# Two PSUM banks for the turned rows of the output projections, three projection weights loaded a stage ahead, another load order in the second attention, and the gate terms of the mLSTM moved into the first attention

## Chip, cores and metric

The kernel runs on 1 core of a Trainium2 chip, as one launch. The metric is the device time of that launch in microseconds (us); smaller is better.

## What is computed

Two transformer blocks, one after the other, on 2048 tokens of width 1024, all in float32. Only the parts that the change touches are given.

```python
# first block: windowed attention and a two-way mLSTM side by side, one output projection, expert-choice FFN
att = latent_attention(q, k, v, k_ctx, v_ctx, sink)        # 8 heads, blocks of 128, window 128, 256 context keys
st_f = mlstm_state_update(zero, cmk, cmv, cli_f, clf_f)    # two context chunks give the first state, each way
h_sum = bidir_mlstm(mq, mk, mv, li_f, lf_f, li_b, lf_b, st_f, st_b)      # 16 chunks of 128 tokens each way
mix = concatenate([att, mlstm_out(h_sum, mo, mlstm_norm_w)])
x = x + g1 * (mix @ w_out)                                 # w_out 1024 x 1024
hx2 = modulate(rmsnorm(x, norm2_w), sh2, sc2)              # goes to the router and the experts
# mLSTM state step
b = cumsum(lf); w = b[-1] - b + li; m_new = max(b[-1] + m, w.max())
C_new = exp(b[-1] + m - m_new) * C + einsum('s,sd,sv->dv', exp(w - m_new), k, v)
# second block
proj = h @ w_in                                            # w_in 1024 x 1472
attn = mla_attention(...)                                  # 4 heads, causal, 2048 x 2048, head width 128 + 64
x = x + gate1 * (concatenate([rms_norm(attn), rms_norm(lru)]) @ w_out)
h2 = rms_norm(x, norm2_g) * (1 + scale2) + shift2          # router and 32 experts follow
```

## The kernel before

The program is a row of stages, each with its own buffers and a barrier of all engines at its end: `inp1` (first projection), `att` (windowed attention), `ml` (mLSTM), `out1` (first output projection), `choose` (expert choice), `moe1`, `inp2` (second projection), `lata` (second attention), `out2`, `route`, `moe2`. In every stage each engine has its instruction stream written out in Python, and semaphores set the order between the streams. SP issues nearly all loads, in the order in which they are written; POOL issues the stores.

**Output projections** (`out_projection`, used for `out1` and `out2`). The 2048 tokens are 16 tiles of 128 rows. For a tile t, PE multiplies the turned mixed rows `mixT` by `w` into `psO` (L1889, 16 matmuls, each in two passes in the trace). DVE adds the residual and normalizes into `xn`; PE turns `xn` by eight 128x128 transposes into `psX` (L1907), four (one "half") into the single bank at a time; ACT evicts each half with scale and shift into `h2T` (L1873); PE multiplies `h2T` by the router weights (`psL`, L1915). One step of the PE stream is: product of tile n+1, turn of the mixed rows of tile n+2 (`psM`), router product of n-1, turn of `xn` of tile n. The second half of a tile waits until ACT has evicted the first:

```python
for q in range(2):
    if not (isinstance(t, int) and t == 0 and q == 0):
        pe.wait_ge(h2T_ready, 2 * t + q)
```

The stage loads `w` itself: eight DMAs of 512 KB on SP, then the router weights `wr` and the gate row `gr`, all on one semaphore `w_landed`, for which the first product waits.

**mLSTM.** `GateColumns` computes, from the 16 gate columns of all 18 chunks (`gate_rows`, left in SBUF by `inp1`), cumulative sums, running maxima and exponents: `chain` on DVE, `products` on PE, `exponents` on ACT, at the start of the stage `ml`. The four context steps (two chunks, both ways) then follow one another through one PSUM tile `psC` and the state `C`, and then the 32 steps of the scan.

**First attention.** Per block of 128 queries and per group g of four: scores in `psS` (single buffer), a minimum on DVE (L1173), exp on ACT (L1218), turn on PE (`psP`), product with values (`psO`). The window mask is added in `psS` by two bf16 matmuls of 128 columns for each of the two kv heads (L1100).

**Second projection** (`inp2`) loads its own `w_in` (six DMAs) after the first rows of x, then some 19 small parameter loads on semaphore `fixed`; the first product waits for all of them (L3078). **Second attention** (`lata`) loads per head seven pieces on one semaphore and starts its scores (L3234) when all seven are there.

Of the kernel before, what the change touches and what calls it, by code (L numbers as in the profile page):

```python
# [250 lines left out]
def first_modulation(nc, K, results, c, vectors, w_mod, b_mod, norm1, first_weights):  # L251
# [4 lines left out]
    with Stage(nc, "mod1") as s:  # L256
# [51 lines left out]
        def _(dve):  # L308
# [11 lines left out]
            dve.wait_ge(scaled, NV)  # L320

# [628 lines left out]

class ChunkRows:
# [16 lines left out]
def window_attention(nc, K, tm1, qT, kT, sink, att_out, chunk_rows):  # L968
# [8 lines left out]
    with Stage(nc, "att") as s:  # L977
# [20 lines left out]
        psO = s.ps("psO", [P, BANK])  # L998
        fill, cut, masked, fixed = s.sem("fill"), s.sem("cut"), s.sem("masked"), s.sem("fixed")
# [38 lines left out]
        def _(sp):  # L1038
            sp.dma_start(kc[:, :], kT[:, 0:CTX]).then_inc(fixed, 16)
# [17 lines left out]
            for c in range(NBLK, chunk_rows.n):  # L1057
                chunk_rows.load(sp, c)

        @block.gpsimd  # L1060
        def _(pool):
            pool.memset(wide[:, :, :, :], 0.0).then_inc(fill, 1)
# [23 lines left out]
        def _(pe):  # L1086
            def scores(n, j, g):
# [52 lines left out]
            def body(n, j):  # L1140
                for g in range(G):
# [20 lines left out]
        def _(dve):  # L1162
            dve.wait_ge(fixed, 48)
# [39 lines left out]
            bound(0, 0, 0)  # L1203
            blocks(dve, body)
# [3 lines left out]
        def _(act):  # L1208
# [15 lines left out]
            def body(n, j):  # L1224
                for g in range(G):
# [10 lines left out]
                    if g in (1, 2) and late(n, 1):  # L1236
                        if g == 1 and late(n, 2):
# [3 lines left out]
                                   ).then_inc(keptA, 1)  # L1241
            exp(0, 0, 0)
            blocks(act, body)
# [5 lines left out]

class GateColumns:  # L1250

# [5 lines left out]
    def __init__(self, nc, s, K, g, b_gates, banks):  # L1257
# [3 lines left out]
        self.cols = s.sb("g_cols", [P, 5, 2, NC, H])  # L1261
# [29 lines left out]
    def give_rows(self, sp, rows, row_landed):  # L1291

        sp.wait_ge(self.neg_ready, 1)
        for d in range(2):
            sp.dma_start(rows[d * self.NC:(d + 1) * self.NC, :].rearrange("n (h t) -> n h t", h=self.H), self.neg[:, d, :]
                         ).then_inc(row_landed, 16)
# [9 lines left out]
    def products(self, pe):  # L1306
# [18 lines left out]
        mm.then_inc(rowed, 1)  # L1325
        pe.wait_ge(scanned, 4)
# [2633 lines left out]
```

## Time and profile before

| | |
|---|---|
| runs of the kernel | 4604.95, 4609.95, 4611.72 us; median 4609.95 us |
| profiled execution | 4612.13 us, span 4610.5 us |
| PE busy | 4054.4 us, 88% of the span |
| DVE busy | 1743.2 us, 38% |
| ACT busy | 1451.5 us, 31% |
| POOL busy | 568.2 us, 12% |
| mean DMA rate | 126 GB/s |
| PE in `att`, `ml` (us from the start of the span) | 781.9 to 1074.7, 1086.5 to 1275.5 |
| PE in `out1`, `out2` | 1293.7 to 1634.2, 3588.2 to 3929.4 |
| PE in `inp2`, `lata` | 2505.4 to 3048.2, 3083.1 to 3573.1 |

PE is the engine that is busy for most of the span; what it does not do is either idle time ahead of an instruction, which the trace puts down to a releaser, or time in which its clock is granted at half rate (1.2 instead of 2.4 GHz; the windows give the mean grant as PEclk). Both are read by stage.

### The profile page before, as it was taken

To read this page: it belongs to the slowest core of one execution; us is meant where nothing else is said; L and a number is where in the kernel's file an instruction comes from. 1 tells how busy PE (TensorE), PEld (TensorE's weight loads), DVE (VectorE), ACT (ScalarE), POOL (GpSimd) and SP (SyncE) were. 2 spreads that over 40 slices of the span, in tenths; PEclk is the share of its full clock that TensorE was granted. 3 is DMA by queue.
4 is the path that set the end of the run, shared out by engine and by line. 5 is a ranking of instruction groups with operands and counts; after the bars stand their busy time and mean duration, and the time that the engine had idled before them with its cause. 6 is when DMAs were issued, how large, how long until landed. Compare 5 with 4: busy or idle time off the path is not lost. (4 is left out here: it accounts for less than half of the span.)

```text
span 4610.5 us, 54913 instructions
## 1 busy us (share of the span) xinstructions
PE 4054.4 (88%) x18100; PEld 2515.4 (55%) x18101; DVE 1743.2 (38%) x3720; ACT 1451.5 (31%) x3214; POOL 568.2 (12%) x716
## 2 busy tenths in 40 slices
PE   7999997997979968999996999948898799499998
PEld 4676765555834426767674777725555344233333
DVE  1433434664544350010101677743333333433332
ACT  1121222553433311111111566632222122244443
POOL 0000001001500011111010000000000000123333
PEclk8999998998989969999998999969999899699999
DMA  6112212224143547555553121141110332488873
GB/s 233 70 63 87 81 71 89 75 79 117 54 170 124 212 148 252 171 189 176 183 172 109 44 66 63 46 119 49 47 25 10 139 110 81 173 288 284 288 223 73
DMA packets 229921, 582.56 MB, mean 126 GB/s; under 512 B 30006, under 2 KB 100807, under 8 KB 213371
## 3 DMA queue, kind: packets, MB, share of 16 engines
q1 hardware_dynamic: 177690, 395.98, 25.0%
q0 software_dynamic: 52064, 184.48, 13.3%
q8 instruction: 91, 1.49, 0.1%
q14 instruction: 76, 0.61, 0.0%
HBM read 437.88 MB, written 142.42 MB: 126 GB/s over the span
## 5 line engine op out<-in xcount | busy, mean ns | idle before, releaser
L1889 PE MATMUL out_psO<-out_w,out_mixT 128*128 128x512 f32 x1024 | 490.1, 640 | 19.4 <-DMA out_gr<-mod_out 17.7
L863 PE MATMUL inp_psU<-inp_w,inp_hT 128*128 128x512 f32 (+3 forms) x1376 | 420.8, 464 | 0.0
L1889 PEld LDWEIGHTS out_psO<-out_w,out_mixT 128*128 128x128 f32 x1024 | 208.8, 207 | 280.4 <-issue 261.8
L3716 PE MATMUL moe_psU<-moe_wu,moe_xT 128*64 x768 | 348.4, 607 | 7.2 <-issue 6.3
L3718 PE MATMUL moe_psU<-moe_bu,moe_xT 128*64 128x512 f32 x768 | 348.5, 607 | 0.0
L863 PEld LDWEIGHTS inp_psU<-inp_w,inp_hT 128*128 128x128 f32 x1376 | 256.0, 190 | 152.7 <-issue 122.5
L859 PE MATMUL inp_psU<-inp_hT,inp_w 128*128 128x256 f32 x1088 | 244.2, 385 | 9.3 <-DVE inp_tm L665 4.5
L3078 PE MATMUL inp_psU<-inp_hT,inp_w 128*128 128x256 f32 x1024 | 230.6, 382 | 17.4 <-DMA inp_wg<-in_lru_wx 17.4
L2376 PE MATMUL moe_psD<-moe_d_w,moe_hT 128*128 128x512 f32 x512 | 236.6, 622 | 0.9 <-DVE moe_hT L2418 0.9
L2360 PE MATMUL moe_psG<-moe_xT,moe_g_w 128*128 128x256 f32 x1024 | 233.0, 381 | 4.6 <-DMA moe_u_w<-in_w_up 4.6
L2360 PE MATMUL moe_psG<-moe_xT,moe_u_w 128*128 128x256 f32 x1024 | 231.5, 379 | 0.0
L859 PEld LDWEIGHTS inp_psU<-inp_hT,inp_w 128*128 128x128 f32 x1088 | 208.0, 193 | 41.3 <-issue 3.9
L3078 PEld LDWEIGHTS inp_psU<-inp_hT,inp_w 128*128 128x128 f32 x1024 | 195.3, 192 | 50.7 <-issue 24.8
L3716 PEld LDWEIGHTS moe_psU<-moe_wu,moe_xT 128*64 128x64 f32 x768 | 103.2, 139 | 214.3 <-issue 214.3
L2400 ACT ACTIVATE moe_sg<-moe_psG 128x256 f32<-128x256 f32 x64 | 24.6, 384 | 618.9 <-PE moe_psG L2360 618.9
L2360 PEld LDWEIGHTS moe_psG<-moe_xT,moe_g_w 128*128 128x128 f32 x1024 | 195.5, 191 | 38.2 <-issue 7.2
L2360 PEld LDWEIGHTS moe_psG<-moe_xT,moe_u_w 128*128 128x128 f32 x1024 | 194.6, 190 | 26.5
L3234 PE MATMUL lata_psS<-lata_kn,lata_qn 128*128 128x512 f32 (+3 forms) x320 | 146.0, 573 | 56.5 <-DMA lata_kr<-lotsT 34.9
L2418 DVE TENSOR_TENSOR moe_hT<-moe_sg,moe_psG 128x256 f32<-128x256 f32 x64 | 27.0, 421 | 427.4 <-ACT moe_sg L2400 427.4
L3264 PE MATMUL lata_psO<-lata_v,lata_pT 128*128 128x128 f32 x1088 | 146.3, 281 | 33.0 <-DVE lata_pT L3290 21.0
L3694 PE MATMUL moe_psD<-moe_wd,moe_hT 128*64 x384 | 172.7, 592 | 1.3 <-ACT moe_hT L3756 1.3
L3697 PE MATMUL moe_psD<-moe_bd,moe_hT 128*64 128x512 f32 x384 | 172.7, 592 | 0.0
(598 smaller groups left out, 6637.6 us busy)
## 6 DMA issues: line engine op xcount, KB each, us to landing
moe_wu<-in_w_up SPq DMA_DIRECT2D x32, 2048.0 KB, 13.2
moe_g_w<-in_w_gate SPq DMA_DIRECT2D x16, 2048.0 KB, 8.3
moe_u_w<-in_w_up SPq DMA_DIRECT2D x16, 2048.0 KB, 13.2
moe_d_w<-in_w_down SPq DMA_DIRECT2D x16, 2048.0 KB
moe_wd<-in_w_down SPq DMA_DIRECT2D x32, 1024.0 KB, 15.2
mod_w<-in_w_ada SPq DMA_DIRECT2D x24, 1024.0 KB, 7.0
inp_mod_w<-in_w_mod SPq DMA_DIRECT2D x16, 1024.0 KB, 4.9
xn<-out_xn POOLq DMA_DIRECT2D x32, 512.0 KB
```

Source lines behind the costliest of these rows:

```text
L859: mm = pe.matmul(psU[:, u % NB, 0:G], w[:, k, fm_lo + u * P:fm_lo + (u + 1) * P], hT[:, par, k, :], start=(k == 0), stop=(k == KD - 1))
L863: mm = pe.matmul(psU[:, u % NB, 0:n], hT[:, par, k, j * P:(j + 1) * P], w[:, k, lo:lo + n], start=(k == 0), stop=(k == KD - 1))
L1889: mm = pe.matmul(psO[:, j, h, :], mixT[:, j, k, :], w[:, k, h * BANK:(h + 1) * BANK], start=(k == 0), stop=(k == KD - 1))
L2360: mm = pe.matmul(psG[:, f % 2, at_col:at_col + N], w[:, j, k, f * P:(f + 1) * P], xT[:, p, k, :], start=(k == 0), stop=(k == KD - 1))
L2376: mm = pe.matmul(psD[:, b, :], hT[:, f, r * P:(r + 1) * P], d_w[:, j, f, h * BANK:(h + 1) * BANK], start=(f == 0), stop=(f == FB - 1))
L3078: mm = pe.matmul(psU[:, m % 2, u % 2 * G:(u % 2 + 1) * G], w[:, k, TM2_W + u * P:TM2_W + (u + 1) * P], hT[:, par, k, :], start=(k == 0), s ...
L3234: pe.matmul(flat[:, at + c:at + c + m], qn[:, j, t * P:(t + 1) * P], kn[:, j, c:c + m], start=True, stop=False)
L3264: mm = pe.matmul(psO[:, n % 2, :], pT[:, u % 2, c % 4, :], v[:, j, c, :], start=(c == 0), stop=(c == tile_of[n]))
L3694: pe.matmul(psD[0:HALF, n, :], hT[:, p, f, 0:HALF], wd[:, bass.ds(slot, 1), f, c].rearrange("p a n -> p (a n)"), start=(f == 0), stop=(f = ...
L3697: mm = pe.matmul(psD[HALF:P, n, :], hT[:, p, f, HALF:P], bd[:, p, f, c], start=(f == 0), stop=(f == FB - 1), tile_position=(0, HALF))
L3716: pe.matmul(psU[0:HALF, p, :], xT[:, p, k, 0:HALF], wu[:, bass.ds(slot, 1), k, :].rearrange("p a n -> p (a n)"), start=(k == 0), stop=(k = ...
L3718: mm = pe.matmul(psU[HALF:P, p, :], xT[:, p, k, HALF:P], bu[:, p, k, :], start=(k == 0), stop=(k == KD - 1), tile_position=(0, HALF))
```

## The change

1. `psX` gets two banks, one for each half of a tile; a half now waits for the eviction of the same half of the tile before.
2. `w_out` of `out1` is held in two halves: the first is loaded by SP at the end of `ml`, the second in `out1`. For `out2` both halves are loaded at the end of `lata`. The first product waits for each half where it first uses it; `wr` and `gr` have semaphores of their own, waited for by the router product and by DVE. `w_in` of `inp2` is loaded by SP at the end of `moe1`.
3. In `lata`, SP loads kn, kr, qr, kr, qr, qn and then v; v has a semaphore of its own, waited for ahead of the head's first product with v. The loads of an odd head wait until v of the even one has landed.
4. The gate terms run in `att`: a first part ahead of the first scores, the rest behind them. PSUM banks for them are those of `psP`, so that the first turn waits for their end. `ml` keeps only the steps: its first scores come first, and the two context chunks of each way are added up in PSUM (their weights are scaled to one reference in one more DVE operation), so that two sums and two copies stand in place of four sums and four updates.
5. The two mask matmuls of a kv head are one with 2x128 columns.

```diff
@@ out_projection @@
-        psX = s.ps("psX", [P, BANK])
+        psX = s.ps("psX", [P, 2, BANK])
...
-                    if not (isinstance(t, int) and t == 0 and q == 0):
-                        pe.wait_ge(h2T_ready, 2 * t + q)
+                    if not (isinstance(t, int) and t == 0):
+                        pe.wait_ge(h2T_ready, 2 * t + q - 1)
                     for k in range(4 * q, 4 * q + 4):
-                        mm = pe.transpose(psX[:, (k % 4) * P:(k % 4 + 1) * P], xn[:, j, k * P:(k + 1) * P], K["ident"][:, :])
+                        mm = pe.transpose(psX[:, q, (k % 4) * P:(k % 4 + 1) * P], xn[:, j, k * P:(k + 1) * P], K["ident"][:, :])
...
-                if isinstance(t, int) and t == 0:
-                    pe.wait_ge(w_landed, 16 * (KD + 2))
...
+                        if isinstance(t, int) and t == 0 and h == 0 and k % 4 == 0:
+                            pe.wait_ge(out_weights.landed[k // 4], 32)
...
-                    for k in range(KD):
-                        sp.dma_start(w[:, k, :], w_out[k * P:(k + 1) * P, :]).then_inc(w_landed, 16)
-                    sp.dma_start(wr[:, :, :], w_router).then_inc(w_landed, 16)
-                    sp.dma_start(gr[:, :], gate_row.to_broadcast([P, D])).then_inc(w_landed, 16)
+                    out_weights.load_rest(sp)
+                    sp.dma_start(wr[:, :, :], w_router).then_inc(wr_landed, 16)
+                    sp.dma_start(gr[:, :], gate_row.to_broadcast([P, D])).then_inc(gr_landed, 16)
@@ new: OutWeights (out1 with halves=1, out2 with halves=2), EarlyColumns for w_in of inp2 @@
+    def load(self, sp, h):
+        lo = h * KD // 2
+        for k in range(0, KD // 2, 2):
+            sp.dma_start(self.half[h][:, k:k + 2, :], self.view[:, lo + k:lo + k + 2, :]).then_inc(self.landed[h], 16)
@@ second_projection @@
             load(0)
-            for k in range(0, KD, 2):
-                sp.dma_start(w[:, k:k + 2, TM2_W:n_cols], wv[:, k:k + 2, TM2_W:n_cols]).then_inc(w_fm_landed, 16)
-            for k in range(0, KD, 4):
-                sp.dma_start(w[:, k:k + 4, 0:TM2_W], wv[:, k:k + 4, 0:TM2_W]).then_inc(w_tm_landed, 16)
@@ window_attention, PE @@
-                    for c in range(2):
-                        at = LO + c * 2 * P
-                        mm = pe.matmul(psS[:, kv, at:at + P], ident[:, :], mask[:, kind(n), c, :], start=False, stop=(c == 1))
-                    mm.then_inc(scored, 1)
+                    pe.matmul(psS[:, kv, LO:BANK].rearrange("p (c t) -> p c t", t=P)[:, 0:3:2, :], ident[:, :], mask[:, kind(n), :, :],
+                              start=False, stop=True).then_inc(scored, 1)
...
+                else:
+                    pe.wait_ge(gates.argued, 1)
+                    pe.wait_ge(gates.neg_ready, 1)
...
+            products = gates.products(pe)
+            next(products)
             pe.wait_ge(fixed, 48)
             pe.wait_ge(masked, 1)
             scores(0, 0, 0)
+            next(products, None)
@@ mlstm, PE @@
+            def grow_context(x):
...
+                for h in range(H):
+                    pe.matmul(bank(psC, h), wk_first[:, x, h, :], v[:, chunk(x), h, :], start=True, stop=False)
+                    mm = pe.matmul(bank(psC, h), wk[:, x, h, :], v[:, chunk(2 + x), h, :], start=False, stop=True)
...
-            for u in range(U0):
-                grow(u)
             for u in range(U0, NU + 1):
                 if u < NU:
                     scores(u)
+                if u == U0:
+                    for x in range(2):
+                        grow_context(x)
```

In the PE stream at the start of `att` (scores are L1092 before and L1139 now), before:

```order
L1092 MATMUL att_psS<-att_kw,att_q 128x384 x2
L1095 MATMUL att_psS<-att_kc,att_q 128x256 x2
L1100 MATMUL att_psS<-att_mask,att_ident 128x128 x4
```

and now:

```order
L1386 MATMUL att_psP<-att_g_f,tri_le 128x72
L1387 MATMUL att_psP<-att_g_f,ones 128x72
L1386 MATMUL att_psP<-att_g_f,tri_ge 128x72
L1387 MATMUL att_psP<-att_g_f,ones 128x72
L1392 MATMUL att_psP<-ident,ml_cols 72x128
L1392 MATMUL att_psP<-att_g_turn,ml_cols 72x128
L1139 MATMUL att_psS<-att_kw,att_q 128x384 x2
L1142 MATMUL att_psS<-att_kc,att_q 128x256 x2
L1145 MATMUL att_psS<-att_mask,att_ident 128x2x128 x2
L1397 MATMUL att_psP<-ident,att_g_pm 128x72 x2
L1400 MATMUL att_psP<-att_g_dg,ones 128x72 x2
```

The gate products stand ahead of the first scores and between them and the next ones, where PE had only waited.

In the PE stream at the start of `ml`, before (`psC` are the context sums, `psR` and `psS` the scores of the first step):

```order
L1318 MATMUL ml_psN<-ml_g_f,tri_le 128x72
L1319 MATMUL ml_psN<-ml_g_f,ones 128x72
L1318 MATMUL ml_psN<-ml_g_f,tri_ge 128x72
L1319 MATMUL ml_psN<-ml_g_f,ones 128x72
L1324 MATMUL ml_psR<-ident,ml_g_cols 72x128
L1324 MATMUL ml_psR<-ml_g_turn,ml_g_cols 72x128
L1328 MATMUL ml_psS<-ident,ml_g_pm 128x72 x2
L1331 MATMUL ml_psQ<-ml_g_dg,ones 128x72 x2
L1334 MATMUL ml_psQ<-ml_g_back,ml_g_turn 128x72
L1337 MATMUL ml_psR<-ident,ml_g_mx 72x128 x2
L1543 MATMUL ml_psC<-ml_v,ml_wk 128x129 x16
L1555 MATMUL ml_psR<-ml_rows,ident 128x512
```

and now:

```order
L1633 MATMUL ml_psR<-ml_rows,ident 128x512
L1634 MATMUL ml_psR<-ml_mask,ml_ident 128x512
L1640 MATMUL ml_psS<-ml_q,ml_kT 128x128 x4
L1611 MATMUL ml_psC<-ml_v,ml_wk_first 128x129
L1612 MATMUL ml_psC<-ml_v,ml_wk 128x129
```

The scores of the first step are the first work of the stage, and the 16 context matmuls follow in pairs.

In the SP stream at the start of `lata`, the loads of the first head, before:

```order
L3209 DMA lata_qn<-lotsT 128x2048
L3210 DMA lata_kn<-lotsT 128x2048
L3211 DMA lata_v<-v 128x16x128
L3216 DMA lata_qr<-lotsT 64x2048
L3218 DMA lata_kr<-lotsT 64x2048
L3216 DMA lata_qr<-lotsT 64x2048
L3218 DMA lata_kr<-lotsT 64x2048
```

and now:

```order
L3277 DMA lata_kn<-lotsT 128x2048
L3280 DMA lata_kr<-lotsT 64x2048
L3282 DMA lata_qr<-lotsT 64x2048
L3280 DMA lata_kr<-lotsT 64x2048
L3282 DMA lata_qr<-lotsT 64x2048
L3284 DMA lata_qn<-lotsT 128x2048
L3285 DMA lata_v<-v 128x16x128
```

v went from third to last, and it is no longer one of those that the scores wait for.

## Rows read from the trace of the kernel before

**Rows 1.** Waits of PE over the span: us in total, times, longest.

```profile
PE out_psX L1907 <- ACT out_h2T L1873: 51.4, 32, 1.7
```

**Rows 2.** Windows: stretch, length, busy us of each engine, PEclk, DMA share, GB/s.

```profile
892.00:1050.00 158.00, 147.36 (x1010) 83.94 (x1008) 96.18 (x226) 94.02 (x244) 6.77 (x9) 1.00 0.26 82
1320.00:1337.00 17.00, 14.99 (x41) 7.08 (x42) 10.64 (x17) 5.93 (x11) 1.08 (x2) 1.00 0.48 170
1357.00:1597.00 240.00, 222.32 (x709) 114.81 (x707) 104.48 (x166) 88.89 (x175) 12.82 (x24) 0.92 0.40 148
3650.00:3890.00 240.00, 220.76 (x697) 113.11 (x696) 87.90 (x142) 50.64 (x142) 19.27 (x36) 0.92 0.29 104
```

**Rows 3.** Timeline of PE in `out1`: start, duration, idle time before and releaser.

```profile
1320.29 13.97 PE L1889 MATMUL out_psO<-out_w,out_mixT 128*128 128x512 f32 x32 [0.78 <-ACT out_mixT L1864]
...
1457.20 15.60 PE L1889 MATMUL out_psO<-out_w,out_mixT 128*128 128x512 f32 x32
...
1477.00 0.66 PE L1907 MATMUL out_psX<-ident,out_xn 128*128 128x128 f32 x4 [1.60 <-ACT out_h2T L1873]
```

**Rows 4.** Window over the start of one product in `out1`, columns as in rows 2.

```profile
1457.30:1460.50 3.20, 3.20 (x5) 1.21 (x4) 0.00 (x0) 3.06 (x6) 0.00 (x0) 0.50 0.97 357
```

**Rows 5.** Timeline at the starts of `out1` and `out2`.

```profile
1294.88 0.60 ACT L1864 ACTIVATE out_mixT<-out_psM 128x512 f32<-128x512 f32 x1 [3.88 <-PE out_psM L1898]
...
1303.18 15.90 PE L1889 MATMUL out_psO<-out_w,out_mixT 128*128 128x512 f32 x32 [8.34 <-DMA out_gr<-mod_out]
...
3589.33 0.60 ACT L1864 ACTIVATE out_mixT<-out_psM 128x512 f32<-128x512 f32 x1 [6.79 <-PE out_psM L1898]
...
3598.65 2.07 PE L1889 MATMUL out_psO<-out_w,out_mixT 128*128 128x512 f32 x2 [9.35 <-DMA out_gr<-mod_out]
```

**Rows 6.** Timeline at the start of `inp2`.

```profile
2498.12 0.83 SPq L2556 DMA_DIRECT2D inp_x<-x  x2
...
2506.54 5.71 ACT L2819 ACTIVATE inp_hT<-inp_psT,mod_cols,mod_scale 128x128 f32<-128x128 f32 x16 [1.87 <-PE inp_psT L2993]
...
2510.51 0.50 SPq L2575 DMA_DIRECT2D inp_iv<-in_inv  x1
...
2522.06 1.00 SPq L2588 DMA_DIRECT2D inp_wg<-in_lru_wx  x1
...
2528.01 4.57 PE L3078 MATMUL inp_psU<-inp_hT,inp_w 128*128 128x256 f32 x10 [17.40 <-DMA inp_wg<-in_lru_wx]
```

**Rows 7.** DMA issues in `lata` from 3060.5 to 3061.5 us (median us to landing).

```profile
lata_kn<-lotsT SPq DMA_DIRECT2D x1, 1024.0 KB, 7.4
lata_v<-v SPq DMA_DIRECT2D x1, 1024.0 KB, 11.8
```

**Rows 8.** Timeline at the start of `lata`.

```profile
3060.63 0.34 SPq L3210 DMA_DIRECT2D lata_kn<-lotsT  x1
3061.18 0.45 SPq L3211 DMA_DIRECT2D lata_v<-v  x1
...
3083.07 1.21 PE L3234 MATMUL lata_psS<-lata_kn,lata_qn 128*128 128x512 f32 x1 [34.90 <-DMA lata_kr<-lotsT]
```

**Rows 9.** Timeline at the starts of `att` and `ml`.

```profile
775.29 0.34 SPq L1039 DMA_DIRECT2D att_kc<-kT  x1
...
781.88 1.65 PE L1092 MATMUL att_psS<-att_kw,att_q 64*128 64x384 f32 x4 [15.10 <-DMA att_vc<-tm]
...
787.53 1.65 PE L1092 MATMUL att_psS<-att_kw,att_q 64*128 64x384 f32 x4 [2.60 <-ACT att_p L1218]
...
1079.65 0.35 SPq L1289 DMA_DIRECT2D ml_g_bg<-in_b_gates  x1
...
1090.03 0.64 PE L1324 MATMUL ml_psR<-ml_g_turn,ml_g_cols 128*72 128x128 f32 x2
...
1111.49 2.07 PE L1555 MATMUL ml_psR<-ml_rows,ident 36*128 36x512 f32 x2
...
1123.02 1.06 PE L1543 MATMUL ml_psC<-ml_v,ml_wk 128*128 128x129 f32 x8
```

More of the change, by code:

```diff
@@ L320, in _, with __init__, load @@
             dve.wait_ge(scaled, NV)
+class EarlyColumns:
+    def __init__(self, nc, stack, name, w_in, n_fm):
+        self.w = stack.enter_context(nc.sbuf_tensor(name, [P, KD, w_in.shape[1]], F32))
+        self.view, self.first = w_in.rearrange("(k p) n -> p k n", p=P), w_in.shape[1] - n_fm
+        self.fm_landed, self.tm_landed = nc.alloc_semaphore(f"{name}_fm_landed"), nc.alloc_semaphore(f"{name}_tm_landed")
+    def load(self, sp):
+        for k in range(0, KD, 4):
+            sp.dma_start(self.w[:, k:k + 4, self.first:], self.view[:, k:k + 4, self.first:]).then_inc(self.fm_landed, 16)
+        for k in range(0, KD, 4):
+            sp.dma_start(self.w[:, k:k + 4, 0:self.first], self.view[:, k:k + 4, 0:self.first]).then_inc(self.tm_landed, 16)
 class LateModulation:
@@ L948, in _, with __init__, add, load_ahead @@
             pool.wait_ge(y_stored, 16 * last)
+class OutWeights:
+    def __init__(self, nc, stack, name, w_out, halves):
+        self.nc, self.stack, self.name, self.view = nc, stack, name, w_out.rearrange("(k p) n -> p k n", p=P)
+        self.half, self.ahead = [], halves
+        self.landed = [nc.alloc_semaphore(f"{name}_landed{h}") for h in range(2)]
+        for h in range(halves):
+            self.add(stack)
+    def add(self, stack):
+        self.half.append(stack.enter_context(self.nc.sbuf_tensor(f"{self.name}{len(self.half)}", [P, KD // 2, D], F32)))
+    def load(self, sp, h):
+        lo = h * KD // 2
+        for k in range(0, KD // 2, 2):
+            sp.dma_start(self.half[h][:, k:k + 2, :], self.view[:, lo + k:lo + k + 2, :]).then_inc(self.landed[h], 16)
+    def load_ahead(self, sp):
+        for h in range(self.ahead):
+            self.load(sp, h)
+    def load_rest(self, sp):
+        for h in range(self.ahead, 2):
+            self.load(sp, h)
 class ChunkRows:
@@ L1038, in _ @@
         def _(sp):
+            gates.load(sp)
             sp.dma_start(kc[:, :], kT[:, 0:CTX]).then_inc(fixed, 16)
@@ L1162, in _ @@
         def _(dve):
+            chain = gates.chain(dve)
+            next(chain)
             dve.wait_ge(fixed, 48)
@@ L1203, in _ @@
             bound(0, 0, 0)
+            next(chain, None)
             blocks(dve, body)
@@ L1247, in _, with __init__ @@
                 keep_r(half)
+class StepGates:
+    def __init__(self, nc, stack):
+        n = ROWS // P
+        self.cols = stack.enter_context(nc.sbuf_tensor("ml_cols", [P, 5, 2, n, M_HEADS], F32))
+        self.rows = stack.enter_context(nc.sbuf_tensor("ml_rows", [2 * n, BANK], F32))
+        self.landed = nc.alloc_semaphore("ml_rows_landed")
 class GateColumns:
@@ L1255, with __init__ @@
     W = NC * H
-    def __init__(self, nc, s, K, g, b_gates, banks):
+    def __init__(self, nc, s, K, g, b_gates, banks, steps):
         NC, H, W = self.NC, self.H, self.W
@@ L1517, in put @@
                                ).then_inc(stored[x], 16)
+            pool.wait_ge(chunk_rows.landed, chunk_rows.ALL)
+            for n, to in enumerate((wk_first, wk)):
+                weigh_context(pool, 2 * n + 1, to).then_inc(c_weighted_back, 1)
             for u in range(U0, NU):
@@ L1551, in scores @@
                 else:
-                    pe.wait_ge(row_landed, 32)
-                    pe.wait_ge(setup, 3 + H)
+                    pe.wait_ge(steps.landed, 32)
+                    pe.wait_ge(setup, 2 + H)
                 r = u % 2 * NC + u // 2
@@ L1911, in route @@
                 pe.wait_ge(h2T_ready, 2 * t + 2)
-                if not (isinstance(t, int) and t == 0):
+                if isinstance(t, int) and t == 0:
+                    pe.wait_ge(wr_landed, 16)
+                else:
                     pe.wait_ge(lg_ready, t)
@@ L2293, in _ @@
                     load(i, j, False)
+            next_columns.load(sp)
         @block.gpsimd
@@ L2450, in second_projection @@
     H, LB, TAPS = A_HEADS, L_W // P, 4
-    n_cols = w_in.shape[1]
     NF = FM_COLS // P
@@ L3175, in latent_attention @@
         landed = [s.sem(f"landed{j}") for j in range(2)]
+        v_landed = [s.sem(f"v_landed{j}") for j in range(2)]
         stored = [s.sem(f"stored{j}") for j in range(2)]
```

182 lines of the change are left out of this document (94 added, 88 removed).

## Prediction

> **What bounds the kernel now.** I read the page first: PE is busy for 88% of the span, so time can be won only where PE idles or runs at half clock. The second view is the list of PE's waits [rows 1]: the longest in total is that of the second four transposes of `psX` for ACT's eviction of the first four, 51.4 us in 32 waits of 1.6 to 1.7 us, one for each of the 32 tiles of the two output projections. The third view is the granted clock by window [rows 2]. Both output projections run at 0.92, while the windowed attention, whose PE also waits again and again (147.36 of 158 us busy), keeps 1.00, and so do the first tiles of `out1`. The fourth is the timeline of one tile [rows 3]: the product of 32 passes lasts 13.97 us at 1320 and 15.60 us at 1457, and the window over the beginning of the slow one shows a grant of 0.50, that is 1.2 GHz [rows 4]. Just ahead of it PE did router matmuls of 16 columns, four transposes, and nothing for 1.6 us. So each tile pays twice: the wait, and a piece at half clock behind it. What is left are stage starts: products that wait for weights [rows 5], for a tail of small loads [rows 6], for seven loads of a head [rows 8], and the gate chain ahead of the mLSTM [rows 9].
>
> **Two banks.** The second half needs the bank that ACT emptied a tile ago. 31 waits of 1.65 us vanish; in the last tile of each stage only the router product is behind, which needs both evictions (two groups on ACT, in series, about as long as the wait each), and of its wait about 1 us stays: 51.4 − 2 = 49.5 us. Does the wait turn up elsewhere? A tile's product is followed by the turn of the mixed rows, the router product and `psX`; DVE has 104.48 of 240 us of work and ACT 88.89 [rows 2], under half each, and everything that the next product needs from them was made during the product before. A tile of 20.0 to 20.5 us would become one of 17.1. DVE's work per tile is 104.48/12 = 8.7 us plus its round trips to ACT, which fits.
>
> **The clock.** If the wait is what makes the clock fall, it no longer falls: the product returns from 15.60 to 13.97, 1.63 us a tile [rows 3]. The mean of 0.92 over two times 240 us gives the same from the other side: 0.08 x 480 = 38 us. I take 24 tiles x 1.63 = 39 us. What speaks for it: before the router products begin, the wait of 1.7 us alone cost no clock [rows 2], and in the attention waits of this size do not either; it takes the wait and the narrow router matmuls together, and the change takes one of them away. What speaks against: the narrow matmuls stay. Bounds: 0 and 42.
>
> The Trainium skill, "TensorE: Matmul & The Clock Gate", section "A second HAM failure mode: psum-queue depth-cycling", says that short idles between groups of matmuls can make the clock swing between its two levels; the rows at 0.92 agree. The same page's section "HAM oscillation — how this bites in real kernels" tells of a kernel in which double-buffering PSUM brought no further gain. By it this part would be worth nothing and the time would be 4470 + 49.5 + 39 = about 4558 us; here the trace has the wait on the one bank by name, 32 times, so I go by the rows.
>
> **Weights of the projections.** In `out1` the first product started at 1303.18, and its rows were ready at 1294.88 + 0.60 = 1295.5 [rows 5]. Half of `w` is there from before, and the other half, four 512 KB pieces' worth instead of eight, is needed four matmuls later. Gain 7.7 us. In `out2` rows were ready at 3589.9 and the product started at 3598.65: 8.7 us, and the norm weights, whose load also had `w` beside it, may land a little earlier; I take 9 us. The loads themselves now stand behind the last loads of `ml` and `lata` on SP, where nothing waits on SP. In `inp2` the small loads stood behind six of `w`: the first of them past the block was issued at 2510.51, the last at 2522.06, 1.0 long, and the product came 5.0 us after that [rows 6]. Without `w` they start at 2498.95: 2498.95 + 12.55 + 4.95 = 2516.5 if issue is what limits them; the other floor is `hT`, ready at 2506.54 + 5.71 = 2512.25. I take 2515, a gain of 13 (11.5 to 15.8). The cover of the moved `w_in` is the end of `moe1`, whose own loads are all issued ahead of it.
>
> **Second attention.** v is 1 MB in short rows; it landed at 3061.18 + 11.8 = 3073.0, kn before it at 3060.63 + 7.4 = 3068.0 [rows 7, 8]. The queue works one load after the other, so v took 5.0 us of it. Six loads in place of seven ahead of the first scores: 3083.07 − 5.0 = 3078.1, gain 5 us. v then lands at about 3083, and between the first scores and the first product with v lie the minimum, the exp and the turn, which cover 5 us. The odd head's loads now wait for v, some 12 us later than before, and have a whole head of cover (490 us of `lata` for four heads, 122 each).
>
> **Gate terms.** In `ml`, PE reached the first scores at 1111.49, that is 31.8 us after the stage's first load, at half clock [rows 9]; the state sum at 1123.02 is the first at full clock, 43.4 us in. Now the first scores need the mask (estimated at 3 us) and the first q and k (six first loads of `att` took 781.88 − 775.29 = 6.6 us, so say 4.5 for two): scores until 7.5; the context sums take 4 x 1.06 = 4.2 us warm and 8.5 cold, say 6 with the turn of the clock; one copy between the two sums 1.1; the second scores, the read of the state and the values 4. That brings the same state sum to 18.5: gain 25 us (19 if all of it stays cold). In `att` the gate products end 1090.67 − 1079.65 = 11.0 us after the load of the bias; from 775.3 that is 786.3, so the first scores come 4.4 us later than 781.88. The second part of the chain then runs on DVE behind the first two minima and ahead of the second scores; by adding its DVE steps (about 3 us until the last product of PE) I get second scores at 794.1 in place of 787.53, 6.6 us. A colder clock at this place may cost 1 to 2 more: 8 us (bounds 4.4 and 16, nothing overlapped). Net 17 us, between 3 and 21.
>
> **Mask matmuls.** One of 256 columns streams as long as two of 128, so the minimum on DVE, which is what waits for it, starts as before: 0, at most 0.05 us in 64 groups, 3 us, either way.
>
> **Sum.** 49.5 + 39 + 7.7 + 9 + 13 + 5 + 17 = 140.2 us. Against the profiled execution: 4612.1 − 140.2 = 4471.9; the median of the runs is 2.2 us below that execution, so 4470 us. It would be 3.0% less.
>
> **Rivals.**
> - The clock falls on every tile in spite of the second bank, since the router matmuls of 16 columns alone are enough. Then 39 us are missing: 4509. For it: the mean of 0.92 leaves about one fall for every tile that has router matmuls. Against: the first fall comes only with wait and router matmuls in the same place. Chance 0.14.
> - The wait on `psX` moves to another buffer of the tile (`mixT`, or DVE's residual chain behind `psO`), tiles stay at 20 us, and only the stage starts gain: 4470 + 88.5 = 4558. Against: DVE and ACT are under half busy. Chance 0.04.
> - Slower: the output stages, with no pause left, get the lower clock for the whole of their product, not for a piece. At 1.2 GHz a product takes about 28 us in place of 14: 32 x 14 = 448 us more, some 4900. It decides against the gain once a third of the product time is at half clock (140 us). Rows 2 speak against it, since the dense stretch from 1320 to 1337, 14.99 of 17 us busy with the same product, is granted 1.00. Chance 0.03.
> - The forecast: 0.79, its own range 4452 to 4488, from the bounds of the gate terms and of `inp2`, and a few falls of the clock in `moe1` more or less, 1.7 us each, as that stage's phase shifts.
>
> The range takes in the first rival: 4450 to 4512. No change can be told from within 0.2% of the median (9 us): chance 0.01. Faster 0.96, slower 0.03.
>
> **What would show it.** After: the row of `psX` waiting for ACT is gone or a few us; PEclk in the middle of both output stages 0.98 or more, and a product of 13.9 to 14.0 us in each tile; tiles 17 us apart; the first product within 1 us behind `mixT` in both; the first product of `inp2` 17 us after the first load instead of 30; first scores of `lata` at 18 instead of 23 us; `ml` shorter by 25 us and `att` longer by 8. Wrong would be: 0.92 kept with the waits gone (first rival), or a new releaser with 1 to 2 us per tile (second).

## The result, and the profile after

| | before | after |
|---|---|---|
| median of the runs | 4608.67 us (4604.95 to 4611.72, 4 runs) | 4449.89 us (4448.3 to 4451.33, 4 runs) |
| profiled execution | 4612.13 us | 4451.26 us |
| PE busy | 88% of the span | 3991.6 us, 90% of 4449.6 us |

The ratio is 0.9659, with a 95% interval of 0.9643 to 0.9674: 158.8 us less, where 140 were forecast. The time lies at the lower edge of the range (4450 to 4512) and 2 us below the forecast's own one. Cutting both traces at the first instruction of each stage gives the place of the gain:

| stage | before, us | after, us | difference | forecast |
|---|---|---|---|---|
| `att` | 304.4 | 310.3 | +5.9 | +8 |
| `ml` | 201.8 | 176.3 | −25.5 | −25 |
| `out1` | 353.8 | 295.8 | −58.0 | −52 |
| `moe1` | 775.2 | 774.5 | −0.7 | 0 |
| `inp2` | 561.4 | 543.3 | −18.1 | −13 |
| `lata` | 518.5 | 512.9 | −5.5 | −5 |
| `out2` | 355.1 | 295.5 | −59.6 | −53 |

(The forecasts of `out1` and `out2` are half of 49.5 + 39 each, with 7.7 and 9 for the start.) The two profiled executions lie 160.9 us apart, a little more than the medians. The stages without a change of their own keep their length within 1 us. Among the kernels of this document whose code for a stage is equal, that stage's length differs by up to 3.1 us in `lata`, 2.8 in `inp2` and 0.8 to 1.6 in `att`, `ml`, `out1` and `out2`; a smaller difference in a stage says nothing.

Windows over the steady tiles of both output stages after the change, columns as in rows 2:

```profile
1300.00:1540.00 240.00, 240.00 (x841) 128.41 (x840) 122.57 (x193) 104.16 (x209) 14.89 (x28) 1.00 0.50 185
3510.00:3750.00 240.00, 240.00 (x841) 128.41 (x840) 104.91 (x168) 58.15 (x167) 22.96 (x43) 1.00 0.34 124
```

Where [rows 2] had 222.32 and 220.76 us of work at a clock of 0.92, PE now works without a gap at the full grant. The timeline of two tiles of `out1`, which answers to [rows 3]:

```profile
1326.03 13.90 PE L1955 MATMUL out_psO<-out_w,out_mixT 128*128 128x512 f32 x32
...
1340.20 1.86 PE L1983 MATMUL out_psL<-out_wr,out_h2T 128*128 128x16 f32 x16
1341.90 1.07 PE L1973 MATMUL out_psX<-ident,out_xn 128*128 128x128 f32 x8
1342.81 13.90 PE L1955 MATMUL out_psO<-out_w,out_mixT 128*128 128x512 f32 x32
```

A tile takes 1342.81 − 1326.03 = 16.78 us. The eight transposes into `psX` stand in one row now, with no idle time ahead of them.

The starts of the other stages, timeline of all engines (of the changed kernel; they answer to [rows 5, 6, 8, 9]):

```profile
776.34 0.34 SPq L1357 DMA_DIRECT2D att_g_bg<-in_b_gates  x1
...
787.62 1.65 PE L1139 MATMUL att_psS<-att_kw,att_q 64*128 64x384 f32 x4
...
794.91 1.65 PE L1139 MATMUL att_psS<-att_kw,att_q 64*128 64x384 f32 x4
...
1086.63 0.40 SPq L1552 DMA_DIRECT2D ml_kT<-conv  x1
...
1104.61 1.06 PE L1621 MATMUL ml_psC<-ml_v,ml_wk 128*128 128x129 f32 x8
...
1275.14 0.60 ACT L1930 ACTIVATE out_mixT<-out_psM 128x512 f32<-128x512 f32 x1 [3.59 <-PE out_psM L1964]
...
1275.84 16.86 PE L1955 MATMUL out_psO<-out_w,out_mixT 128*128 128x512 f32 x32 [0.73 <-issue]
...
2420.71 0.82 SPq L2623 DMA_DIRECT2D inp_x<-x  x2
...
2422.05 0.43 SPq L2638 DMA_DIRECT2D inp_iv<-in_inv  x1
...
2429.12 5.69 ACT L2882 ACTIVATE inp_hT<-inp_psT,mod_cols,mod_scale 128x128 f32<-128x128 f32 x16 [1.87 <-PE inp_psT L3056]
...
2431.55 0.51 SPq L2651 DMA_DIRECT2D inp_wg<-in_lru_wx  x1
...
2434.95 1.62 PE L3141 MATMUL inp_psU<-inp_hT,inp_w 128*128 128x256 f32 x3 [1.77 <-ACT inp_hT L2882]
...
2964.21 0.33 SPq L3277 DMA_DIRECT2D lata_kn<-lotsT  x1
...
2982.38 1.21 PE L3302 MATMUL lata_psS<-lata_kn,lata_qn 128*128 128x512 f32 x1 [29.71 <-DMA lata_qn<-lotsT]
...
3487.46 0.60 ACT L1930 ACTIVATE out_mixT<-out_psM 128x512 f32<-128x512 f32 x1 [5.99 <-PE out_psM L1964]
...
3488.16 16.62 PE L1955 MATMUL out_psO<-out_w,out_mixT 128*128 128x512 f32 x32 [0.73 <-issue]
```

The first products of both output stages start 0.1 us behind `mixT`. That of `inp2` starts 14.2 us after the stage's first load and is released by `hT`, no longer by a load. The first scores of `lata` start 18.2 us after the first load. In `ml` the first state sum at full clock comes 18.0 us in, where it was 43.4. In `att` the second scores come 18.6 us in, where it was 12.2.

Two of PE's waits after the change (us in total, times, longest), and the second of them before it:

```profile
PE moe_psT L2416 <- ACT moe_xT L2459: 29.5, 32, 1.2
...
PE out_psL L1983 <- ACT out_h2T L1939: 9.4, 4, 2.6
```

```profile
PE out_psL L1915 <- ACT out_h2T L1873: 6.4, 4, 1.6
```

The row of [rows 1] is gone. The longest wait that PE repeats is now one of the same kind, in `moe1`: transposes that wait for ACT to empty their bank, 32 times.

### The profile page after: what moved, and what is told of

Same layout as the page of the kernel before. It is cut to its first block and busy times, and to the rows that moved or that the text cites. A ratio compares the mean times of both kernels' runs of the same rounds, so it can differ in the third digit from the quotient of the medians.

```text
span 4449.6 us, 54579 instructions
## 1 busy us (share of the span) xinstructions
PE 3991.6 (90%) x17972; PEld 2492.8 (56%) x17973; DVE 1739.0 (39%) x3704; ACT 1446.1 (32%) x3214; POOL 574.9 (13%) x718
## 5 line engine op out<-in xcount | busy, mean ns | idle before, releaser
L1955 PE MATMUL out_psO<-out_w,out_mixT 128*128 128x512 f32 x1024 | 450.7, 599 | 3.0 <-ACT out_mixT L1930 1.6
L1955 PEld LDWEIGHTS out_psO<-out_w,out_mixT 128*128 128x128 f32 x1024 | 194.1, 192 | 237.6 <-issue 237.6
L3141 PEld LDWEIGHTS inp_psU<-inp_hT,inp_w 128*128 128x128 f32 x1024 | 195.2, 191 | 34.9 <-issue 9.2
L3729 POOL DMA_INDIRECT out_rows<-moe_y,moe_at_out x48 | 126.9, 2643 | 366.7 <-DMA out_rows<-moe_y,moe_at_out 170.0
```

Source lines behind the costliest of these rows:

```text
L1955: mm = pe.matmul(psO[:, j, h, :], mixT[:, j, k, :], out_weights.half[k // 4][:, k % 4, h * BANK:(h + 1) * BANK], start=(k == 0), stop=(k = ...
L3141: mm = pe.matmul(psU[:, m % 2, u % 2 * G:(u % 2 + 1) * G], w[:, k, TM2_W + u * P:TM2_W + (u + 1) * P], hT[:, par, k, :], start=(k == 0), s ...
L3729: pool.indirect_dma_start(out=out, out_offset=bass.IndirectOffsetOnAxis(ap=at_out[:, p, :], axis=0), in_=y[:, p, :], in_offset=None, compu ...
```

## The experiments

**One bank again, and two banks alone.** The theory at this point: the two banks gave some 100 us, partly the wait and partly the clock; the rest came from the starts of the stages. The rival: the loads carried a part of it. Two kernels take the change apart from either side. The edit, taken back from the changed kernel and put into the kernel before:

```diff
-        psX = s.ps("psX", [P, 2, BANK])
+        psX = s.ps("psX", [P, BANK])
...
-                    if not (isinstance(t, int) and t == 0):
-                        pe.wait_ge(h2T_ready, 2 * t + q - 1)
+                    if not (isinstance(t, int) and t == 0 and q == 0):
+                        pe.wait_ge(h2T_ready, 2 * t + q)
```

Expected of the first:

> The changed kernel with the turned rows of both output projections in one bank again, and the old waits with it; all loads and gates stay as changed. If the two banks are what made both output stages shorter by more than their earlier start, each stage becomes some 50 us longer: 58.0 and 59.6 less the 7.7 and 9 of the start, so 4450 + 101 = 4551 us, with a wait of 1.6 us per tile back and a granted clock of 0.92 over the steady tiles. If the loads carried the gain (less traffic in the stage, better spaced tiles), the time stays within 20 us of 4450.

Expected of the second:

> The kernel before with only the turned rows of both output projections over two banks. By the same theory 4609 - 101 = 4508 us, granted clock 1.00 over the steady tiles of both stages, tiles of 16.8 us. If the gain needed the loads too, less than 70 us are gained here; if the parts add up, this one's gain and the loss of the changed kernel with one bank agree within 5 us.

Measured: 4549.04 us with one bank (ratio to the kernel before 0.9873, 0.9856 to 0.9889), 99.2 us above the changed kernel; 4507.1 us with two banks alone (0.9781, 0.9765 to 0.9798), 100.1 us below the kernel before's 4607.22 in the same comparison. In the first, `out1` and `out2` are 7.8 and 9.1 us shorter than before; in the second 51.3 and 49.7, at a granted clock of 1.00 in both. The parts add up, and the loads have no share in the tiles. The tile of the kernel with one bank, timeline of PE, and its windows:

```profile
1386.08 15.32 PE L1955 MATMUL out_psO<-out_w,out_mixT 128*128 128x512 f32 x32
...
1401.66 1.86 PE L1983 MATMUL out_psL<-out_wr,out_h2T 128*128 128x16 f32 x16
1403.37 0.64 PE L1973 MATMUL out_psX<-ident,out_xn 128*128 128x128 f32 x4
1405.60 0.78 PE L1973 MATMUL out_psX<-ident,out_xn 128*128 128x128 f32 x4 [1.59 <-ACT out_h2T L1939]
1406.27 15.54 PE L1955 MATMUL out_psO<-out_w,out_mixT 128*128 128x512 f32 x32
...
1300.00:1540.00 240.00, 220.62 (x704) 114.24 (x703) 107.02 (x169) 90.60 (x179) 12.77 (x24) 0.92 0.36 131
```

From the first transpose to the next product it takes 1406.27 − 1403.37 = 2.90 us; with two banks 1342.81 − 1341.90 = 0.91. So a wait whose idle time is 1.59 costs 1.99 us here. Over both stages, without the last two tiles of each, it costs 1.94 us on average. The part beyond the idle time lies on both sides of it: four transposes in a row take 0.46 us from start to start (half of 0.91), but 0.64 pass from the first of them to the pause, and 0.67 from the first behind the pause to the product. It need not be the clock: the kernel with the short router product, below, has the same 2.90 us in a tile at full clock.

Added up from both traces, from start to start over all 32 tiles, the transposes and what they wait for took 100.4 us with one bank and 41.0 with two, and the products 484.0 and 445.5. So 59.4 us of the difference are the wait and 38.5 the clock.

**Does the wait or do the narrow matmuls lower the clock?** In a tile both lie side by side. One kernel keeps the wait and takes the narrow matmuls nearly away; the other keeps the two banks, and so no wait, and doubles them. The router matmuls have 16 columns in `out1` and 36 in `out2`; they take 1.70 us a tile in both. The edits, the first on top of one bank:

```diff
-                for k in range(KD):
+                for k in range(1):
```
```diff
-                for k in range(KD):
+                for k in 2 * tuple(range(KD)):
```

> The changed kernel with one bank, and the router product cut from eight matmuls of few columns to one (the router's numbers are left out for seven of eight blocks of the rows, so later stages choose other experts; only the two output stages are read). The wait of 1.6 us per tile is kept. If the wait alone lowers the clock, the product takes 15.6 us in most tiles and the granted clock stays near 0.92. If wait and narrow matmuls lower it together, the product takes 13.9 us in every tile, the granted clock is 1.00, and a tile is 20.5 - 1.7 (clock) - 1.6 (seven of eight router matmuls) = 17.2 us.

> The same kernel as the one-bank kernel with the short router product (seven of the eight blocks of rows left out of the router's product, so that later stages choose other experts; only the output stages are read), since the profiled execution of its first run was disturbed from its first stage on. The kernel with doubled router products has shown that 3.6 us of narrow matmuls lower the clock with no wait. If the wait of 1.6 us per tile lowers it by itself too, the product takes 15.6 us in most tiles at 0.92. If not, 13.9 us in every tile at 1.00, and a tile is 17.2 us.

> The changed kernel with its two banks, and the router product made twice, one behind the other (same result). The narrow matmuls double to some 3.7 us per tile, with no wait among them. If they alone can lower the clock when there are enough of them (the prediction's first rival), the product goes to 15.6 us and the granted clock to 0.92: a tile of 16.8 + 1.9 + 1.7 = 20.4 us, +115 us in all. If it takes an idle engine, the clock stays 1.00 and a tile is 16.8 + 1.9 = 18.7 us, +60 us in all.

Of either run of the kernel with the short router product, one of two executions took over 10,000 us, which no other kernel here did. In the first run that was the profiled one, with matmuls 1.9 to 2.4 times as long from the first stage on, far ahead of the edit; nothing is read from it, and its cause stays open. The other executions took 4515.58 and 4512.76 us; the latter is the profiled one of the repeat (its routed experts take 57 us longer, having other rows to do, so only the output stages are read): windows over both stages, and two tiles.

```profile
1300.00:1540.00 240.00, 217.40 (x639) 104.86 (x638) 121.39 (x191) 100.71 (x206) 14.89 (x28) 0.99 0.48 172
3510.00:3750.00 240.00, 217.04 (x639) 104.78 (x638) 104.00 (x167) 56.77 (x167) 21.41 (x41) 0.99 0.33 118
...
1377.84 13.90 PE L1955 MATMUL out_psO<-out_w,out_mixT 128*128 128x512 f32 x32
...
1392.01 0.29 PE L1983 MATMUL out_psL<-out_wr,out_h2T 128*128 128x16 f32 x2
1392.16 0.64 PE L1973 MATMUL out_psX<-ident,out_xn 128*128 128x128 f32 x4
1394.39 0.66 PE L1973 MATMUL out_psX<-ident,out_xn 128*128 128x128 f32 x4 [1.60 <-ACT out_h2T L1939]
1395.06 13.99 PE L1955 MATMUL out_psO<-out_w,out_mixT 128*128 128x512 f32 x32
```

The wait is as it was (51.7 us in 32), the tile takes 1395.06 − 1377.84 = 17.22 us as expected, and the clock is 0.99: in each window it fell in one tile or so, not in every one. So the wait with hardly any narrow matmuls beside it hardly lowers it. With the router product made twice, without any wait, 4540.72 us (0.9853, 0.9833 to 0.9873), 90.8 above the changed kernel, between the two expectations:

```profile
1384.01 15.60 PE L1955 MATMUL out_psO<-out_w,out_mixT 128*128 128x512 f32 x32
...
1399.88 3.64 PE L1983 MATMUL out_psL<-out_wr,out_h2T 128*128 128x16 f32 x32
1403.37 1.07 PE L1973 MATMUL out_psX<-ident,out_xn 128*128 128x128 f32 x8
1404.28 13.90 PE L1955 MATMUL out_psO<-out_w,out_mixT 128*128 128x512 f32 x32
...
1300.00:1540.00 240.00, 240.00 (x898) 138.14 (x896) 108.32 (x172) 89.29 (x179) 12.77 (x24) 0.94 0.37 131
3560.00:3800.00 240.00, 240.00 (x942) 140.62 (x941) 93.73 (x149) 53.68 (x154) 19.24 (x36) 0.96 0.31 109
```

PE is busy for 240 of 240 us and the grant is 0.94 and 0.96: one product takes 15.60 us, the next 13.90. The doubling itself is 3.49 − 1.70 = 1.79 us in a steady tile (start of the router product to start of the transposes). Added up from both traces over both stages, the router products take 66 us more (in the last two tiles of a stage they run largely at half clock), the products 17 and the transposes 9; the last two sums are the clock. So narrow matmuls without a pause can lower the clock, when there are twice as many as in this kernel. The prediction's first rival names a real mechanism, and the changed kernel stays on the good side of it.

One thing these runs leave open: the two edits also change the length of a tile (17.2 and 18.7 us or more, against 20.2 with one bank and 16.8 in the changed kernel), and no run changes the length alone. Whether that has a part in when the clock falls is not shown.

The Trainium skill, "TensorE: Matmul & The Clock Gate", section "A second HAM failure mode: psum-queue depth-cycling", puts such swings down to short idles of PE between groups of matmuls. The trace agrees in part: taking the idle of 1.6 us away raised the grant from 0.92 to 1.00, but the same idle beside hardly any narrow matmuls left 0.99, and no idle at all beside twice as many gave 0.94.

**Where the loads stand.** The changed kernel with all early loads back in their own stage (the first product's wait by halves of the weights kept) and the second attention's loads in the old order (qn, kn and v ahead of kr and qr, and no wait for v), and a second kernel in which that product again waits for everything at once. In `inp2` the columns of `w_in` are loaded behind the small loads here, not ahead of them as in the kernel before. Parts of the edits:

```diff
-        out1_weights = OutWeights(nc, outer, "out1_w", A["w_out"], 1)
+        out1_weights = OutWeights(nc, outer, "out1_w", A["w_out"], 0)
...
-        out2_weights = OutWeights(nc, outer, "out2_w", A["w_out_2"], 2)
+        out2_weights = OutWeights(nc, outer, "out2_w", A["w_out_2"], 0)
...
-            next_columns.load(sp)
...
                 sp.dma_start(wg[:, n, :, :], src.rearrange("h i o -> i h o")).then_inc(fixed, 16)
+            columns_in.load(sp)
```
```diff
+                if isinstance(t, int) and t == 0:
+                    for sem, n in ((out_weights.landed[0], 32), (out_weights.landed[1], 32), (wr_landed, 16), (gr_landed, 16)):
+                        pe.wait_ge(sem, n)
...
-                        if isinstance(t, int) and t == 0 and h == 0 and k % 4 == 0:
-                            pe.wait_ge(out_weights.landed[k // 4], 32)
```

> The changed kernel with all three weights loaded within their own stage again (the output weights still in four pieces each, waited for by halves), and the second attention's loads in the old order. Read by stage. By the prediction's working out1 gets longer by 7.7 us, out2 by 9 us, inp2 by 18 us (what it was shorter by), lata by 5.5 us: 4450 + 40 = 4490 us. If the early loads took as much from the stages ahead as they gave (moe1, first and second attention side by side with a large transfer), moe1 and lata get shorter here and the time changes by under 20 us. If two landed halves in place of one full wait is what counts, out1 gets longer by only some 4 us.

> The kernel with all three weights loaded in their own stage, and now the first output product waits as before the change: for both halves of the weights, the router's weights and the gate row at once. With the wait by halves the first product stood 1.9 us (out1) and 2.9 us (out2) in its wait for the weights, before the change 8.3 and 9.4 us. If the split of the wait gave this, both stages get 6.5 us longer: 4470 + 13 = 4483 us. If the fewer and larger transfers gave it, the waits stay at 2 to 4 us and the time at 4470.

Measured: 4470.05 us (0.9691, 0.9677 to 0.9706), 20 above the changed kernel and not 40; and 4484.4 us (0.973, 0.9713 to 0.9746), 14.4 above that. By stage, as difference to the kernel before: `out1` −57.6 and −50.5, `out2` −56.1 and −49.8, `inp2` −4.2 and −4.9, `lata` −2.1 and −1.9. The first products, of the kernel with old loads first, then of that with the full wait (timeline of PE; idle time in brackets):

```profile
1276.58 3.71 PE L1955 MATMUL out_psO<-out_w,out_mixT 128*128 128x512 f32 x4 [1.86 <-DMA out_w<-in_w_out]
...
3507.49 2.90 PE L1955 MATMUL out_psO<-out_w,out_mixT 128*128 128x512 f32 x3 [2.89 <-DMA out_w<-in_w_out]
```

```profile
1285.29 5.12 PE L1956 MATMUL out_psO<-out_w,out_mixT 128*128 128x512 f32 x7 [8.53 <-DMA out_gr<-mod_out]
...
3522.42 4.61 PE L1956 MATMUL out_psO<-out_w,out_mixT 128*128 128x512 f32 x5 [9.59 <-DMA out_gr<-mod_out]
```

The four larger transfers do not shorten the wait: with the full wait it is 8.53 and 9.59 us, where the eight transfers of the kernel before had 8.34 and 9.35. With all loads in the stage, not waiting for everything is worth 57.6 − 50.5 = 7.1 us in `out1` and 6.3 in `out2`. In the kernel with the full wait the first half of the weights of `out1` landed at 1278.29, the second at 1283.46 and the gate row at 1284.93 (3515.20, 3520.35 and 3522.06 in `out2`). So about 5 us of each are the second half of the weights, and the other 1.5 to 1.7 the router's weights and the gate row.

The early load on top of that gives 0.4 us in `out1` (58.0 − 57.6, less than equal stages differ) and 3.5 in `out2`. In `out1` it does bring the first product 1.75 us nearer to the start of the stage, but that product takes 16.86 us there and 15.72 in the kernel with old loads. It lies between 15.6 and 16.9 in kernels with equal loads too, so the 0.4 is not a measure of the early load. The kernel that loads ahead and still waits for everything was not run. By the landings in the changed kernel, its first product would start with `mixT` in `out2`, where all has landed by then (the gate row at 3486.78, `mixT` at 3488.06), and 2.6 us behind it in `out1` (1278.39 and 1275.74). So the two remedies hide largely the same time, and the gain can't be given to one of them.

In `inp2` the product waited 14.91 us for the columns, and against that order the early load is worth 18.1 − 4.2 = 13.9 us, give or take 3. The lengths of `lata` are too close to read, but its start is not: in the kernel with old loads the first scores waited 34.52 us, as before the change, though v has its own semaphore here too; so it is the place of v in the row of loads that gives 34.52 − 29.71 = 4.8 us (29.3 to 29.9 in the kernels with the new order, 33.4 to 34.9 with the old). Timeline of PE in this kernel:

```profile
2999.60 3.77 PE L3298 MATMUL lata_psS<-lata_kn,lata_qn 128*128 128x512 f32 x4 [34.52 <-DMA lata_qr<-lotsT]
```

**The mask in one matmul.** The mask added by two matmuls of 128 columns again:

```diff
-                    pe.matmul(psS[:, kv, LO:BANK].rearrange("p (c t) -> p c t", t=P)[:, 0:3:2, :], ident[:, :], mask[:, kind(n), :, :],
-                              start=False, stop=True).then_inc(scored, 1)
+                    for c in range(2):
+                        at = LO + c * 2 * P
+                        mm = pe.matmul(psS[:, kv, at:at + P], ident[:, :], mask[:, kind(n), c, :], start=False, stop=(c == 1))
+                    mm.then_inc(scored, 1)
```

> The changed kernel with the mask of the first attention's scores added by two matmuls of 128 columns per head pair again, in place of one of 256 strided columns. The prediction put this at 0: the attention stage stays within 1 us of 310.3, the time within 0.1%. Rival: a matmul's start costs some 0.06 us that the wide one saves, 2 x 64 x 0.06 = 8 us longer, which would explain why the stage grew by 5.9 us and not by 8.

Measured: 4454.19 us (0.9655, 0.9641 to 0.9668), the same as the changed kernel. The stage `att` took 310.6 us, 0.3 more. In the traces the four matmuls of 128 columns of a group take 0.234 us from the first start to the next instruction, the two wide ones 0.229, so there is hardly a start to save. The wide mask is worth nothing that can be told, and so the 5.9 us of `att` are the gate chain's.

**The same remedy in the first experts.** The wait of `moe1` shown above has the form of the one that the change took away. There all eight banks are taken, so a second pair cannot be had; but the sixteen transposes of a unit can be issued in two groups, the second one between the two row blocks of the down product:

```diff
-                    turn(*after(i, j, 1))
+                    turn(*after(i, j, 1), (0,))
...
                         mm.then_inc(lowered, 1)
+                    if left and r + 1 < J:
+                        turn(*after(i, j, 1), (r + 1,))
```

> The changed kernel with one more edit, in the first experts: the two row blocks of the next unit are turned apart, the first ahead of the down product's first row block and the second ahead of its second, so that no transpose waits for its bank to be copied out. If the waits for the turned rows' bank (29.5 us, 32 of them) and the nine falls of the clock behind them (1.7 us each) are a real cost, as in the output stages, the time goes to 4450 - 29.5 - 15 = 4405 us. If the falls have another cause, 4420 us. Rival: the wait moves to the products' bank or to the activation engine's copies, since the second copies now end closer to the next up product: 4450 us.

Measured: 4409.12 us (4406.09 to 4413.48; 0.9561, 0.9548 to 0.9574), 40.8 below the changed kernel, with 45 forecast; `moe1` is 43.4 us shorter. One unit of the changed kernel, and its window over `moe1`:

```profile
1789.23 1.04 PE L2416 MATMUL moe_psT<-ident,moe_xg 128*128 128x128 f32 x8
1791.43 0.66 PE L2416 MATMUL moe_psT<-ident,moe_xg 128*128 128x128 f32 x4 [1.16 <-ACT moe_xT L2459]
1792.82 0.66 PE L2416 MATMUL moe_psT<-ident,moe_xg 128*128 128x128 f32 x4 [0.74 <-ACT moe_xT L2459]
1793.31 15.60 PE L2445 MATMUL moe_psD<-moe_d_w,moe_hT 128*128 128x512 f32 x32
...
1700.00:2340.00 640.00, 615.09 (x2423) 447.66 (x2424) 65.83 (x124) 97.91 (x272) 75.68 (x81) 0.98 0.58 187
```

and of the kernel with the split turn:

```profile
1782.25 1.04 PE L2417 MATMUL moe_psT<-ident,moe_xg 128*128 128x128 f32 x8
1783.51 7.13 PE L2446 MATMUL moe_psD<-moe_d_w,moe_hT 128*128 128x512 f32 x16 [0.23 <-DVE moe_hT L2490]
1790.48 1.04 PE L2417 MATMUL moe_psT<-ident,moe_xg 128*128 128x128 f32 x8
1791.35 7.03 PE L2446 MATMUL moe_psD<-moe_d_w,moe_hT 128*128 128x512 f32 x16
...
1700.00:2340.00 640.00, 637.69 (x2587) 471.52 (x2586) 70.62 (x133) 106.64 (x290) 79.14 (x84) 1.00 0.60 192
```

A unit's transposes took 1793.31 − 1789.23 = 4.08 us; now (1783.51 − 1782.25) + (1791.35 − 1790.48) = 2.13. For 16 units that is 31 us, and the grant of 1.00 in place of 0.98 gives the other 12 (0.02 x 640 = 13); added up from the traces, the transposes took 32 us less and the down products 12. This stage has no narrow matmuls at all (256 and 512 columns, and the transposes' 128): here two pauses of 1.16 and 0.74 us among sixteen transposes were enough to lower the clock now and then.

## Why the prediction was right

- **What bounds the kernel, and rows 1 to 4:** right. The wait, and the piece at half clock behind it, were 49.7 to 51.3 us per output stage.
- **Two banks, 49.5 us: mis-sized.** The wait did not turn up elsewhere, which the kernel with one bank shows. But its price was taken from the idle time (1.65), and it costs 1.94 on average from start to start. Over both stages the wait was worth 59.4 us, 10 more than the 49.5, and that is with the last tiles in it: there the wait for `out_psL` grew from 6.4 to 9.4 us, where the prediction allowed 2. A tile became one of 16.78 us and not 17.1.
- **The clock, 39 us: right.** The products took 38.5 us less over both stages. The two stages gain 100.7 us by the kernel with one bank (58.0 − 7.8 + 59.6 − 9.1); the wait and the clock make 97.9 of it. The reason given ("it takes the wait and the narrow router matmuls together") fits the runs with either of them nearly gone, with two limits: enough narrow matmuls do it without a wait, and in `moe1` pauses do it now and then without narrow matmuls.
- **The Trainium skill's word on double-buffering PSUM** ("TensorE: Matmul & The Clock Gate", "HAM oscillation — how this bites in real kernels", where one kernel had no further gain from it), taken over to this one, would have made the time 4558. Two banks alone measured 100.1 us less: the measurement decides, and what told the case apart was that the trace named one bank's eviction as the releaser of each pause.
- **Starts of `out1` and `out2`, 7.7 and 9: right** in size (7.8 and 9.1 by the kernel with one bank). The working gave the gain to the early load. The runs show that not waiting for everything gives 7.1 and 6.3 us with no early load at all, so the two changes overlap, and that the early load on top adds 0.4 and 3.5.
- **Start of `inp2`, 13: mis-sized.** The first product was put at 2515, between two floors and nearer to the later one, the issue of the small loads, 12.55 us long and 4.95 to the product. Without the columns ahead of them they were issued in 10.0 us (2422.05 to 2432.06) and landed within 3, at the same moment as `hT` was complete, so that both floors met at the earlier one: first product 29.9 − 14.2 = 15.7 us sooner, the end of the range given (15.8). What is left of the stage's 18.1, 2.4 us, is not explained; the same stage of the kernel with one bank, whose code is equal, was 1.9 us longer.
- **`lata`, 5: right** (the wait at its start 34.90 before [rows 8], 29.71 after). The place of v gives 4.8 us of it by the kernel with the old order. PE has no wait for the even head's v or for the odd head's loads after the change.
- **Gate terms:** `ml` 25, right, with the state sum at 18.0 us where 18.5 was worked out. The 3 us for the mask came from no row; the first product of `ml` stood 3.1 us behind the stage's first load, released by the mask. `att` 8, mis-sized: the second scores come 6.3 us later (6.6 worked out), and the 1 to 2 us added for a colder clock did not come; 5.9.
- **Mask, 0: right.**

The two profiled executions differ by 160.9 us, 20.7 more than the sum of 140.2: 12 come from the output stages (10 of them the wait, the rest not placed), 5 from `inp2`, 2 from `att`, and between 1 and 2 from the rest. The medians differ by 158.8. All the larger misses went the same way, so the time came out at the edge of the range: the parts were placed rightly, and two of them were priced too low.

## What to carry to other kernels

A short wait that PE repeats costs its start-to-start time, not its idle time, and in this kernel, with narrow matmuls or transposes beside it, a stretch at 1.2 GHz behind it as well: 1.6 us of idle cost 3.1 to 3.4 us in a tile. When no bank is free for double-buffering, move the second group of transposes behind a product that needs nothing from it. Before a weight is loaded a stage ahead, split the wait for it and see what is left to hide: in the output stages that was 0.4 to 3.5 us, in the second projection, where the columns would otherwise land behind all other loads of the stage's start, 13.9.

## What the runs showed of the hardware

- The granted clock of TensorE with 1.70 us of matmuls of 16 or 36 columns a tile of the output stages is 1.00 without a pause and 0.92 with one of 1.6 us; with 0.15 us of them and the pause it is 0.99; with 3.49 us of them and no pause 0.94 and 0.96.
- A product of 32 passes behind a fall of the clock mostly took up to 15.60 us in place of 13.90, in the output stages and in the experts. Many took only a part of it: from start to start they lie anywhere from 13.7 to 15.5 us. With the router product doubled, the transposes took some of it instead, up to 1.74 us for eight in place of 0.91.
- Eight transposes of 128 columns in one go took 0.91 us from the first start to what follows; with a wait of 1.59 us between the fourth and the fifth they took 2.90, which is 0.4 us more than the idle time.
- The small loads of `inp2` were issued on SP in 10.0 us in place of 12.55 and the last landed 2.7 us behind the end of its issue (before, the product that waited for them came 4.95 us behind it) once no large transfer stood among the loads of the stage.
